# A hybrid decoder layer: the input x moved to the head of one DMA queue, and two broadcast rows held back behind a count

## What is computed

```python
mod = jax.nn.silu(c) @ w_ada + b_ada            # c: 1 + 8 conditioning rows; w_ada: 1024 x 6144
sh1, sc1, gt1, sh2, sc2, gt2 = split(mod, 6)
h = rmsnorm(x, g_mix) * (1.0 + sc1) + sh1
z = h @ w_in                                     # 1024 x 2816
q_a, k_a, v_a, q_h, f_h, i_h, g_h = split(z)
o_a = rmsnorm(sink_attention(rotary(q_a), rotary(k_a), v_a), g_attn_out)
lb = cumsum(softmax(hg_lb_logits))[layer]        # lower bound of the forget gate
f = lb + (1.0 - lb) * sigmoid(f_h)
o_h, S_new = hgrn(q_h, 1.0 - f, i_h, log(f))     # gated linear recurrence
x = x + gt1 * (concat(o_a, o_h) @ w_out)
h = rmsnorm(x, g_ffn) * (1.0 + sc2) + sh2
x = x + gt2 * moe(h)                             # top 4 of 32 experts, clamped SwiGLU
y = rmsnorm(x, g_final)
```

## Time and profile before

| what | value |
|---|---|
| median of three runs | 1194.73 us (1193.68 to 1196.06) |
| the profiled execution's own time | 1192.83 us |
| its span, first to last instruction | 1191.0 us |
| TensorE busy | 1102.0 us, 93% |
| VectorE, ScalarE, GpSimd busy | 29%, 14%, 5% |
| moved by DMA | 462.16 MB, mean 388 GB/s |
| mean granted clock of TensorE | 0.994 |

### The profile page before, as it was taken

How to read it: one execution, slowest core, us unless ns; L and a number is a source line. 1 busy time by engine, 2 the same in 40 slices (tenths; PEclk the granted TensorE clock), 3 DMA queues, 4 the chain that set the end, 5 groups by cost and what they waited for, 6 DMA issues and landing times.

```text
span 1191.0 us, 14032 instructions
## 1 busy us (share of the span) xinstructions
PE 1102.0 (93%) x5473; PEld 445.3 (37%) x5473; DVE 350.7 (29%) x752; ACT 163.8 (14%) x314; POOL 56.7 (5%) x88
## 2 busy tenths in 40 slices
PE   5999999999999999989898989898989898989896
PEld 3777756643233333323232322232223222322222
DVE  1636267342312213222222221222122212221224
ACT  2332161311010001000100010001000100000002
POOL 3400000210000000000000000000000000000000
PEclk9999999999999999999999999999999999999999
DMA  9971289999999999999999999999999999999994
GB/s 360 342 282 71 76 360 346 351 358 413 428 424 428 424 428 428 427 425 429 428 425 426 428 428 426 426 429 428 425 426 428 428 426 426 428 428 425 425 429 182
DMA packets 50024, 462.16 MB, mean 388 GB/s; under 512 B 6529, under 2 KB 9793, under 8 KB 19258
## 3 DMA queue, kind: packets, MB, share of 16 engines
q1 hardware_dynamic: 42978, 444.16, 89.8%
q0 software_dynamic: 5760, 13.65, 3.2%
q10 hardware_dynamic: 1256, 3.94, 0.9%
HBM read 460.81 MB, written 5.78 MB: 392 GB/s over the span
## 4 chain that ended last, share of the span: by engine, by line
PE 58%; DMA 39%; DVE 2%; issue 1%; ACT 0%; SPq 0%; ACTq 0%; DVEq 0%
PE bank L1489 27%; DMA arena<-in_w_up 17%; DMA ring<-in_w_up 17%; PE bank L1369 6%; PE bank L1511 4%; PE bank L965 3%; DMA arena<-in_w_down 3%; PE bank L1282 3%; PE bank L864 3%; PE bank L942 3%; PE bank L1482 2%; PE bank L888 1%; PE bank L1038 1%; PE bank L1022 1%; PE bank L1375 1%; DMA x<-in_x_sample 1%
## 5 line engine op out<-in xcount | busy, mean ns | idle before, releaser
L1489 PE MATMUL bank<-arena 128*64 128x512 f32 x1024 | 239.9, 600 | 16.1 <-DMA arena<-in_w_up 15.4
L1489 PE MATMUL bank<-ring,arena 128*64 128x512 f32 x1024 | 241.7, 604 | 13.7 <-DMA ring<-in_w_up 12.7
L1489 PEld LDWEIGHTS bank<-arena 128*64 128x64 f32 x1024 | 67.2, 136 | 169.1 <-issue 149.7
L1489 PEld LDWEIGHTS bank<-ring,arena 128*64 128x64 f32 x1024 | 66.4, 137 | 168.8 <-issue 139.4
L1511 PE MATMUL bank<-arena 128*64 128x512 f32 x512 | 114.8, 596 | 10.4 <-DMA arena<-in_w_down 10.4
L1511 PE MATMUL bank<-ring,arena 128*64 128x512 f32 x512 | 114.6, 596 | 7.3 <-DMA ring<-in_w_down 6.8
L2033 DVE TENSOR_SCALAR arena<-bank 128x256 f32<-128x256 f32 x64 | 24.2, 419 | 280.9 <-PE bank L1489 280.9
L1369 PE MATMUL bank<-arena,mods 128*128 128x512 f32 (+1 forms) x204 | 93.7, 630 | 0.9 <-DVE arena L2060 0.9
L818 ACT ACTIVATE arena<-arena 128x512 f32<-128x512 f32 x32 | 20.2, 630 | 502.5 <-DVE arena L2033 502.5
L2022 DVE TENSOR_TENSOR x<-x,bank 128x512 f32<-128x512 f32 x64 | 44.0, 687 | 147.8 <-PE bank L1369 147.8
L864 PE MATMUL bank<-const,arena 128*128 128x128 f32 (+3 forms) x348 | 50.5, 284 | 20.8 <-DMA ring<-in_w_down 7.9
(11 more groups left out here) (328 smaller groups left out, 789.3 us busy)
## 6 DMA issues: line engine op xcount, KB each, us to landing
ring<-in_w_up SPq DMA_DIRECT2D x64, 2048.0 KB, 34.5
arena<-in_w_up SPq DMA_DIRECT2D x64, 2048.0 KB, 34.4
ring<-in_w_down SPq DMA_DIRECT2D x32, 2048.0 KB, 34.1
arena<-in_w_down SPq DMA_DIRECT2D x32, 2048.0 KB, 33.8
ring<-in_w_ada SPq DMA_DIRECT2D x24, 1024.0 KB, 12.3
ring<-in_w_in SPq DMA_DIRECT2D x4, 2048.0 KB, 23.2
ring<-in_w_in SPq DMA_DIRECT2D x3, 1024.0 KB, 13.4
arena<-in_state_hgrn POOLq DMA_DIRECT2D x8, 256.0 KB, 10.8
```

What stands on the lines that cost most here:

```text
L1489: mm = pe.matmul(B[2 * e + c % 2][64 * a:64 * a + 64, :], lhsT=xTe[:, k, 64 * e:64 * e + 64], rhs=big(PER * s + n)[:, r, 512 * c:512 * (c ...
```

## The change

x is no longer issued by ScalarE. SyncE issues it behind c and ahead of w_ada, the decode rows first and then the two prompt tiles. The two lower-bound rows move on GpSimd from ahead of the sinks to behind the router bias, and wait there for five used chunks of w_ada.

```diff
@@ SyncE
             sp.dma_start(crow[0:1, :], A["c_prompt"]).then_inc(sem("c_full"), 16)
             sp.dma_start(crow[1:9, :], A["c_sample"]).then_inc(sem("c_full"), 16)
+            sp.dma_start(x[0:NB, 2, :], A["x_sample"].rearrange("b s d -> (b s) d")).then_inc(sem("x_full_in"), 16)
+            for t in range(2):
+                sp.dma_start(x[:, t, :], A["x_prompt"][0, P * t:P * (t + 1)]).then_inc(sem("x_full_in"), 16)
             for k in range(N_ADA):
                 room(k)
                 sp.dma_start(chunk(k), w_ada[k, :, 0:CH]).then_inc(full[place(k)], 16)
@@ GpSimd
-            pool.dma_start(lbl[:, 0, :], wide(A["hg_lb_logits"][0:1, :], 0, P)).then_inc(sem("rows_full"), 16)
-            pool.dma_start(lbl[:, 1, :], wide(A["hg_lb_logits"][1:2, :], 0, P)).then_inc(sem("rows_full"), 16)
             pool.dma_start(sinkb, wide(A["attn_sinks"][0:1, :], 0, P)).then_inc(sem("sinks_full"), 16)
...
             pool.dma_start(brout[0:E, :], A["b_router"].rearrange("a e -> e a")).then_inc(sem("sinks_full"), 16)
 
+            pool.wait_ge(chunks_used, 5)
+            pool.dma_start(lbl[:, 0, :], wide(A["hg_lb_logits"][0:1, :], 0, P)).then_inc(sem("rows_full"), 16)
+            pool.dma_start(lbl[:, 1, :], wide(A["hg_lb_logits"][1:2, :], 0, P)).then_inc(sem("rows_full"), 16)
             pool.wait_ge(chunks_used, N_ADA)
@@ ScalarE
             act.dma_start(const[:, 0:NEARLY], A["const"][:, 0:NEARLY]).then_inc(sem("ident_full"), 16)
-            act.dma_start(x[:, 0, :], A["x_prompt"][0, 0:P]).then_inc(sem("x_full_in"), 16)
-            act.dma_start(x[:, 1, :], A["x_prompt"][0, P:S]).then_inc(sem("x_full_in"), 16)
-            act.dma_start(x[0:NB, 2, :], A["x_sample"].rearrange("b s d -> (b s) d")).then_inc(sem("x_full_in"), 16)
             act.wait_ge(sem("c_full"), 32)
```

## The result

The changed kernel takes 1198.03 us (median of 20 runs, 1194.6 to 1201.51) against 1194.86 us (20 runs, 1192.2 to 1198.06): a ratio of 1.003, with a 95% interval of 1.002 to 1.004. It is 3.2 us slower. The prediction was no change (1194.2, 1191.3 to 1197.6); the time lies above its range.

What follows compares the result with a forecast made beforehand. A full weight stream bounds the long expert part, so only an earlier start helps: w_in at 52.6 us starts qh0 at 52.7 instead of 53.2, 0.5 us faster, 1194.2 us against the median 1194.73; range 1191.3 to 1197.6.

Steps and rivals of the forecast that it cites:

- The last chunk of w_ada: Chunk k = 7, the last TensorE needs before L942: landing at 30.2 us instead of 30.5, within 29.7 to 31.0.
- The start of L943: L942 before the change, ahead of qh0 on TensorE: predicted to start at 34.5 us instead of 35.46.
- The lower-bound rows landed in time: GpSimd's rows, first read by L1588: landing near 34.5 us, free up to about 39; rival of late rows, chance 0.04.
- a wait on w_in ahead of qh0: At qh0 (L965), TensorE ready at 52.2 us waits for w_in at 52.6; qh0 starts at 52.7, 0.5 us faster.
- the stream's lag at w_in: SyncE's stream up to w_in: late by 0.5 us for the late start; the rows' move worth nothing there.
- the late start: Start of SyncE's stream, with x issued behind c: costs 0 to 0.7 us, taken as 0.5.
- The fifth chunk: Fifth chunk of w_ada: landing at 21.7 us instead of 22.5, from 1.3 us less for rows and 0.5 late start.
- the price of a lag: At w_in's double chunk: 0.5 us of late start counted as 0.5 us of later landing.
- the double chunk: First double chunk of w_in, which qh0 reads: landing at 52.6 us, between 51.9 and 53.1, instead of 51.9.
- the states' earlier start: GpSimd's state loads start 1.0 us earlier, ahead of w_in: costs 0 to 0.5 us, taken as 0.2.
- The rival of the clock: TensorE at half clock from L914: L914 takes 7.2 us, L942 begins at 38.3, 2.8 us slower, 1197.5; chance 0.13.
- The margin: Ahead of qh0 in the kernel before: w_in's double chunk lands at 51.9 us, qh0 starts at 53.20, 1.3 us later.

Runs made afterwards that it cites:

- with the broadcast late: Only the attention sinks' broadcast moved behind the b_ada rows: in the changed kernel, ratio 1.001; in the kernel before with only the lower-bound rows held back, 0.9999.
- rows alone: Kernel before with only the lower-bound rows held back to five used chunks of w_ada, x still issued by ScalarE: 1199.02 us, ratio 1.0044.
- The kernel before with the states held: Kernel before with GpSimd's state loads, and what follows on its queue, held until the double chunk of w_in has landed: 1192.45 us, ratio 0.9987.

## Why the prediction was wrong

**What held.** x landed at 6.7 us (6.5 to 7 predicted) and bought nothing by itself. The last chunk of w_ada landed at 30.9 (29.7 to 31.0). The start of L943, 35.20, was 0.7 us later than predicted. The lower-bound rows landed in time. In the first profile the wait on x was replaced by a wait on w_in ahead of qh0, as forecast. So the prediction named the right wait; its size was wrong, and with it the sign of the change.

**The first step that failed is the stream's lag at w_in.** The prediction let the stream be late by the late start alone, 0.5 us, and gave the rows 1.3 us ahead of the fifth chunk and nothing at w_in. The fifth chunk, put at 21.7, landed at 22.45 in the profile and at 21.5 to 22.3 in the four other profiles with the same code up to there. That it came near is luck: with the broadcast late it landed at 20.1 and 20.2, so the rows' leaving gave more than 1.3 us, and the stall took most of it back. What the stall took was missing when the rows returned: the first chunk of w_in landed at 34.1 to 35.0, 0.6 to 1.4 us later than before, where the term was 0.5. I costed what leaves the queue and not what moves up in it: the sinks, ten small loads, came forward by 1.1 us in issue and lost their place behind 0.52 MB of rows, and their broadcast stalled the engines. The prediction named the sinks only as what stands ahead of the new wait. Without that broadcast there, rows alone costs nothing (0.9999). The premise behind this was that full engines are an unchanged stream. They are not: the DMA share of 10 to 14 us was 0.98 at 273 GB/s. (The share of 0.98 to 1.04 that the prediction quotes is 1.05 in one of its own rows.)

**The second step, and the larger, is the price of a lag: the double chunk at 52.6 predicted, 56.6 in the profile** (52.9, 53.9 and 54.8 in the three others). The sum knew that the states would stand ahead of w_in. It took each us of lag as one us of landing, and the states' earlier start of 1.0 us as 0.2 us, with no row for how the queues share the engines. Over the thirteen profiles a us of lag is 3.1 us of landing, and states a us sooner are 2.1. By that line, the prediction's own 0.5 us of late start and 1.0 us of earlier states would have put the landing near 55.6 (an estimate: 51.9 + 1.6 + 2.1). The prediction gave GpSimd's queue at most about half of the bytes and did not name ScalarE's constants there. In the kernel before GpSimd's queue had 54% of the bytes from 38 to 52 us and the constants 23%, which left 24% for SyncE. A row of the queues in that stretch would have shown it; the earlier trace rows gave only the sum of all queues.

**The rival of the clock** was half right. Its place was not: L914 (L915 after) took 4.36 us, not 7.2, with the clock at 0.50 from 19.5 to 26.3, and its end was still early enough. But the half clock came back behind the new wait (1.9 us) and, in the other profile, over L943, which then took 16.50 us and not the 15.85 of the sum. With chunks of w_ada 2.5 us apart the clock fell at 19.5 us in the first profile of the changed kernel, among the bursts; in the second it stayed full through them and fell at 30.9 us, when TensorE had waited 2.58 us for the last chunk. The kernel that the prediction cites from the Trainium skill, "TensorE: Matmul & The Clock Gate", section "HAM oscillation — how this bites in real kernels", starts every burst at the half clock; these two profiles agree only in that a train of bursts can bring it.

**The margin** of 1.3 us rested on one execution. The kernel before with the states held gained 0.13%, which suggests that it was not there in all of them.

## What to carry to other kernels

When a transfer leaves a queue, cost what moves up into its place as well as what is saved. Where two or three queues load at once, read the rate of the one that is needed, not the sum: a chunk that is still on its way when other queues start pays any lag several times over, and holding back the loads that nobody needs yet was worth more here than the order of the ones that are needed. A busy share near 1 does not say that the bytes still flow; read the GB/s beside it. A margin read from one profile is one sample.

## What the runs showed of the hardware

- A broadcast of 32 B to 128 partitions, 4 KB in sixteen packets, took 0.02 us a packet (median) behind 0.52 MB of other loads at 15 us, and as little at 58 us and later. At 10 to 12 us, without those loads ahead of it, the medians were 0.5 to 1.5 us, and up to 1.9 us. The engines then moved 273 GB/s (the change) and 263 GB/s (rows alone) from 10 to 14 us, against 414 and 401 in the same kernels with the broadcast late, at a busy share of 0.98 to 1.03 throughout. The reason is open.
- With one stream of SyncE (w_in, packets of 1 and 2 KB) beside the states and caches on GpSimd's queue (4 KB) and the constants on ScalarE's (8 KB), SyncE's got 24% of the bytes from 38 to 52 us (1.11 of 4.66 MB) although it had been issued first. SyncE's queue and GpSimd's got equal numbers of packets, 739 each; in the changed kernel 717 and 720, in rows alone 705 and 708.
- In thirteen profiles in which the states are not held, the double chunk landed 18.3 us after their issue and 3.1 us more for each us by which the first chunk of w_in came after that issue (lags of 0.04 to 1.72 us).
- The granted clock of TensorE stood at 0.50 for 10 us on end in seven of the profiles, between 29 and 42 us or between 184 and 198 us, and for some 3 to 7 us in the others; the same kernel showed it at different places from one execution to the next.
